# A hybrid decoder block: sums of squares of keys, queries and recurrence output in one fp32 pass, or in two fp32r passes

## The reference

```python
def rms_norm(x, gain):
    xf = x.astype(jnp.float32)
    xf = xf * lax.rsqrt(jnp.mean(xf * xf, axis=-1, keepdims=True) + EPS)
    return xf.astype(x.dtype) * gain
...
    q = rms_norm(q.reshape(B, S, G, HPG, DH), qk_gain[0]).transpose(0, 2, 3, 1, 4)
...
    k_s = rms_norm(heads(k_s), qk_gain[2])
...
    k_w = rms_norm(heads(k_w), qk_gain[3])
...
    o = rms_norm(o, out_gain.astype(jnp.float32)) * jax.nn.silu(g.astype(jnp.float32).reshape(B, S, HG_HEADS, HG_DV))
```

## Time and profile before

| what | value |
| --- | --- |
| time, median of 3 runs | 806.44 us (805.68 to 806.84) |
| time of the profiled execution | 806.03 us |
| its span, first to last instruction | 804.3 us |
| TensorE busy | 797.1 us (99%), granted clock 0.999 |
| VectorE busy | 396.2 us (49%) |
| ScalarE busy | 196.3 us (24%) |
| GpSimd busy | 489.1 us (61%) |

### The profile page before, as it was taken

One profiled execution on the slowest core, in us unless ns is written; L12 is line 12 of the kernel. 1 busy time (PEld: TensorE's weight loads), 2 busy tenths in 40 slices (PEclk: granted clock), 3 DMA queues, 4 the chain that ended last, 5 costly groups with the idle time before them and its releaser, 6 DMA issues.

```text
span 804.3 us, 12357 instructions
## 1 busy us (share of the span) xinstructions
PE 797.1 (99%) x4632; PEld 635.8 (79%) x4632; DVE 396.2 (49%) x565; ACT 196.3 (24%) x402; POOL 489.1 (61%) x325
## 2 busy tenths in 40 slices
PE   9999999999999999999999999999999999999998
PEld 7788878988787666577888888888888888888886
DVE  5794577734465445633457667661000476650000
ACT  6101753214311445725112222220000122210000
POOL 5666544676454755555666566676666676676663
PEclk9999999999999999999999999999999999999999
DMA  8244222233522010015223223233223223323320
GB/s 282 98 139 154 82 80 80 79 106 105 183 79 78 27 53 28 1 53 183 84 101 104 89 95 104 80 102 105 84 99 104 82 102 104 98 85 131 130 78 26
DMA packets 23549, 78.01 MB, mean 97 GB/s; under 512 B 2723, under 2 KB 3499, under 8 KB 23380
## 3 DMA queue, kind: packets, MB, share of 16 engines
q1 hardware_dynamic: 19964, 69.00, 25.8%
q10 hardware_dynamic: 3544, 8.44, 2.9%
HBM read 75.31 MB, written 4.21 MB: 99 GB/s over the span
## 4 chain that ended last, share of the span: by engine, by line
PE 96%; ACT 1%; POOL 1%; DMA 1%; DVE 1%; issue 0%; SPq 0%; DVEq 0%; POOLq 0%; ACTq 0%
PE bank L385 27%; PE bank L387 26%; PE bank L386 26%; PE bank L709 3%; PE bank L731 3%; PE bank L752 2%; PE bank L467 1%; PE bank L468 1%; PE bank L469 1%; PE bank L409 1%; ACT gates L1081 1%; PE bank L516 1%; DMA x<-in_xT 1%; POOL wsp L305 1%; PE bank L625 1%; PE bank L741 1%
## 5 line engine op out<-in xcount | busy, mean ns | idle before, releaser
L305 POOL TENSOR_TENSOR wsp<-wraw,wsp 128x1024 fp32r<-128x1024 f32 x124 | 305.8, 2466 | 10.3
L303 POOL TENSOR_SCALAR wsp<-wraw 128x1024 fp32r<-128x1024 f32 x124 | 135.3, 1091 | 243.7 <-PE bank L387 159.2
L385 PE MATMUL bank<-hhi,wsp 128*128 128x512 f32 x352 | 140.6, 399 | 0.9 <-POOL wsp L305 0.4
L386 PE MATMUL bank<-hlo,wsp 128*128 128x512 f32 x352 | 137.3, 390 | 0.0
L387 PE MATMUL bank<-hhi,wsp 128*128 128x512 f32 x352 | 137.3, 390 | 0.0
L385 PE MATMUL bank<-ghi,wsp 128*128 128x512 f32 x256 | 100.4, 392 | 0.0
L387 PE MATMUL bank<-ghi,wsp 128*128 128x512 f32 x256 | 99.7, 389 | 0.0
L385 PE MATMUL bank<-uhi,wsp 128*128 128x512 f32 x256 | 99.7, 389 | 0.0
L386 PE MATMUL bank<-glo,wsp 128*128 128x512 f32 x256 | 99.6, 389 | 0.0
L386 PE MATMUL bank<-ulo,wsp 128*128 128x512 f32 x256 | 99.6, 389 | 0.0
L387 PE MATMUL bank<-uhi,wsp 128*128 128x512 f32 x256 | 99.6, 389 | 0.0
(11 more groups left out here) (246 smaller groups left out, 1012.1 us busy)
## 6 DMA issues: line engine op xcount, KB each, us to landing
wraw<-in_w SPq DMA_DIRECT2D x126, 512.0 KB, 3.3
bias_skewed<-bias_lines ACTq DMA_DIRECT2D x1, 2048.0 KB
bias<-bias_skewed ACTq DMA_DIRECT2D x1, 2048.0 KB, 8.7
x<-in_xT ACTq DMA_DIRECT2D x1, 2048.0 KB, 8.1
out<-x ACTq DMA_DIRECT2D x8, 256.0 KB, 2.0
x<-in_xT SPq DMA_DIRECT2D x3, 512.0 KB, 6.6
x<-in_xT SPq DMA_DIRECT2D x2, 256.0 KB, 4.4
wraw<-in_w SPq DMA_DIRECT2D x4, 128.0 KB, 8.0
```

Of the source, the lines that this page charges most:

```text
L303: pool.tensor_scalar(whi[:, two, :], wraw[:, raw, :], 1.0, 0.0, ALU.mult, ALU.add).then_inc(w_hi, 1)
L305: pool.tensor_tensor(wlo[:, two, :], wraw[:, raw, :], whi[:, two, :].bitcast(F32), ALU.subtract).then_inc(w_split, 1)
L385: pe.matmul(out_, wh, mh, start=first, stop=False)
L386: pe.matmul(out_, wh, ml, start=False, stop=False)
```

## The change

The ten sums over 512 columns use fp32r matmuls. ScalarE squares into `sq` as before, waits for that, and copies the square into an fp32r tile `sq_hi` (rounding it). VectorE subtracts: `sq_lo = sq - sq_hi` (`square_low`). TensorE multiplies both by the matrix of ones (now an fp32r copy) into the same bank, the second adding to the first (`split_stat`), and waits for `sq_low` in place of `stat_in`. VectorE's ten subtractions are put in by hand: number n of the first six in turn n of the loop, behind `keep_near(n)` or `keep_32` and ahead of `norm`; 6 and 7 (for `st_o0`, `st_o1`) between `kcn` and `gelu(1)`; 8 and 9 in the loop of the heads. Before the first square ScalarE also waits for `raw_low`, since `sq_hi` lies where `raw_hi` was.

```diff
+            def split_stat(name, matrix):
+
+                i = split_stats[0]
+                pe.wait_ge(sq_low, i + 1)
+                to = claim(name)
+                pe.matmul(to[:], matrix, sq_hi[i // 6][:, i % 2, :], start=True, stop=False)
+                pe.matmul(to[:], matrix, sq_lo[i // 6][:, i % 2, :], start=False, stop=True).then_inc(stat_out, 1)
+                split_stats[0] += 1
...
-            stat("st_ks", pair_ones[:], sq[:, 0, :])
+            split_stat("st_ks", pair_r[:])
...
-                stat(f"st_o{h}", ones[:], sq[:, h % 2, :])
+                split_stat(f"st_o{h}", ones_r[:])
...
+            def square_split(raw):
+
+                i = squares[0]
+                if i >= 2:
+                    act.wait_ge(sq_low, i - 1)
+                if i == 0:
+                    act.wait_ge(raw_low, 2)
+                link(act.activation(sq[:, i % 2, :], raw, ACT.Square))
+                act.activation(sq_hi[i // 6][:, i % 2, :], sq[:, i % 2, :], ACT.Copy).then_inc(sq_high, 1)
                 squares[0] += 1
...
+            dve.tensor_copy(ones_r[:], ones[:])
+            dve.tensor_copy(pair_r[:], pair_ones[:])
...
+            def square_low(i):
+                dve.wait_ge(sq_high, i + 1)
+                dve.tensor_tensor(sq_lo[i // 6][:, i % 2, :], sq[:, i % 2, :], sq_hi[i // 6][:, i % 2, :].bitcast(F32),
+                                  ALU.subtract).then_inc(sq_low, 1)
...
                 if n == 6:
                     keep_64()
+                if n < 6:
+                    square_low(n)
...
             dve.sem_inc(kcn_ready, 1)
+            square_low(6)
+            square_low(7)
             gelu(1)
...
                 dve.tensor_tensor(o_, o_, gs[:, h, :], ALU.mult).then_inc(oa_f, 1)
+                if h < 2:
+                    square_low(8 + h)
```

More of the change, by code:

```diff
@@ L137, in build_block @@
         pt_high = [at("pt_high0", 116.5, [P, 2, 4, 256]), at("pt_high1", 178.5, [P, 2, 4, 256])]
+        ones_r = at("ones_r", 188.5, [P, P], F32R)
+        pair_r = at("pair_r", 189, [P, P], F32R)
+        sq_hi = [at("sq_hi", 190.5, [P, 2, S], F32R), at("sq_hi_o", 194.5, [P, 2, S], F32R)]
+        sq_lo = [at("sq_lo", 172.5, [P, 2, S], F32R), at("sq_lo_o", 198.5, [P, 2, S], F32R)]
         cst = at("cst", 204.5, [P, 336])
@@ L202, in build_block @@
         stat_in = sem("stat_in")
+        sq_high, sq_low = sem("sq_high"), sem("sq_low")
         stat_out = sem("stat_out")
@@ L409, in stat @@
                 pe.matmul(to[:, 0:n], matrix, squares, start=True, stop=True).then_inc(stat_out, 1)
+            split_stats = [0]
+            def split_stat(name, matrix):
[5 more added lines that the diff above has]
+                split_stats[0] += 1
             def first_projection(n, each_k):
@@ L572, in _ @@
             project("kw")
-            stat("st_ks", pair_ones[:], sq[:, 0, :])
+            split_stat("st_ks", pair_r[:])
             near_level(1)
             project("nq0")
-            stat("st_kw", pair_ones[:], sq[:, 1, :])
+            split_stat("st_kw", pair_r[:])
             near_level(2)
             project("nq1")
-            stat("st_q0", pair_ones[:], sq[:, 0, :])
+            split_stat("st_q0", pair_r[:])
             near_level(3)
             project("nq2")
-            stat("st_q1", pair_ones[:], sq[:, 1, :])
+            split_stat("st_q1", pair_r[:])
             near_level(4)
             project("nq3")
-            stat("st_q2", pair_ones[:], sq[:, 0, :])
+            split_stat("st_q2", pair_r[:])
             level_32()
@@ L589, in _ @@
             next(parts)
-            stat("st_q3", pair_ones[:], sq[:, 1, :])
+            split_stat("st_q3", pair_r[:])
             level_64()
@@ L653, in _ @@
             project("ga0")
-            stat("st_o0", ones[:], sq[:, 0, :])
+            split_stat("st_o0", ones_r[:])
             pe.wait_ge(csum, 2)
@@ L828, in _ @@
                     if j == 0:
-                        pe.wait_ge(stat_in, 13)
+                        pe.wait_ge(stat_in, 3)
                         pe.matmul(bank[2][:], ones[:], tmp[:], start=True, stop=True).then_inc(stat_out, 1)
@@ L932, in square @@
                     act.wait_ge(stat_out, squares[0])
-                act.activation(sq[:, squares[0] % 2, :], raw, ACT.Square).then_inc(stat_in, 1)
+                square_split(raw)
+            def square_split(raw):
[6 more added lines that the diff above has]
+                act.activation(sq_hi[i // 6][:, i % 2, :], sq[:, i % 2, :], ACT.Copy).then_inc(sq_high, 1)
                 squares[0] += 1
@@ L1017, in square_o @@
                 act.wait_ge(stat_out, 7 if h < 2 else 7 + h)
-                act.activation(sq[:, h % 2, :], bank[2 + h][:], ACT.Square).then_inc(stat_in, 1)
+                square_split(bank[2 + h][:])
             square_o(0)
```

## The result

| | before | after |
| --- | --- | --- |
| time, median | 806.1 us (6 executions, 805.68 to 806.84) | 814.49 us (6 executions, 813.40 to 817.18) |
| ratio | 1 | 1.0107 (95% interval 1.0092 to 1.0121) |
| profiled execution, its span | 806.03, 804.3 | 813.93, 812.2 |
| mean granted clock | 0.999 (profiled execution) | 0.994 to 0.998 (six executions) |

What follows compares the result with a forecast made beforehand. The prediction took TensorE, busy 797.1 of 804.3 us, to bound the kernel. Keys and queries +2.8, compressed values +1.7 and the other output sums 0 made +4.5: 810.9 us on the median, range 807.4 to 814.2.

Steps and rivals of the forecast that it cites:

- What bounds the kernel: Whole kernel: TensorE, busy 797.1 of 804.3 us, sets the time; VectorE's 49% says nothing about a given moment.
- The price of a pass: Each sum on TensorE: two fp32r matmuls with the switch take 0.55 instead of 0.95, 0.63 after a wait.
- The price of two SBUF inputs: VectorE's subtractions: each waits for the GpSimd operation that runs and makes the next one wait; 0.69 each when unhindered.
- Step 1: Keys and queries: waits of 4.83 for low parts, less 2.00 given back by the sums: +2.8 us.
- Step 2: Compressed values: two low parts push the gelu's second half behind GpSimd's next chunk, so `cmp_v` starts later: +1.7 us.
- Step 3: Last three output sums: no gain, since the next projection waits for the gate's bank that L1154 reads: 0 us.
- The sum: Whole kernel: 2.8 + 1.7 + 0 = +4.5, 810.9 us on the median.
- The rivals: Whole kernel, other outcomes: 801.8 (5%), 807.0 (12%), 808.9 (20%), 813.5 (18%); the forecast itself had 42%.
- The nearest in time, 813.5: Last query's sum: its low part misses the gap between GpSimd operations, VectorE and TensorE wait 2.6 longer: +7.1; 18%.
- Waits grow beyond 0.5 at the third to fifth sum: Keys' and queries' loop, sign of error in step 1: VectorE, not TensorE, would set the pace, norms underrated.

Runs made afterwards that it cites:

- keys alone: Kernel before, with only the six sums of keys and queries as two passes, the output's four left as fp32: 814.56 us, ratio 1.0101.
- output part alone: Kernel before, with only the four output sums as two passes, keys and queries left as fp32: 809.22 us, ratio 1.0031.
- control: Whole change, but the sum `st_q1` waits only for its high part and reads it twice, its low part left out: 817.61 us, ratio 1.0144.
- held sum: Kernel before, fp32 sums kept, with one added wait: `st_q0` also waits for VectorE's norm of the window keys: 807.93 us, ratio 1.0020.
- the last run: Whole change, with `square_low(2)` moved ahead of `advance(2)` and `square_low(7)` behind `gate("ga0")`: 810.81 us, ratio 1.0066.
- the tiny matmuls: Whole change plus 16 tiny fp32 matmuls on TensorE before its first low-part wait, bank claims moved ahead of these waits: 812.46 us, ratio 1.0072.
- one high sum: Whole change, but the sum `st_q0` waits only for its high part and reads it twice, its low part left out: 811.15 us, ratio 1.0067.

## Why the prediction was wrong

**What bounds the kernel**: right. VectorE's share of 49% hid that it was late at a few moments: two waits for low parts, the wait at L677 and a short one at `st_q0`.

**The price of a pass**: right. 0.55 was forecast and the pair with its switch took 0.54 where nothing held it.

**The price of two SBUF inputs**: right. The low part at 198.33 ran only when the L310 of 198.13 had ended, and the low part at 145.97, first by 0.13, made the L310 of 146.10 take 2.79 instead of 2.40. The Trainium skill, page "SBUF — State Buffer", section "Who interferes with whom", has such an exclusive lock; the trace agrees.

**Step 1**: its sum was right, 2.8 forecast and 2.6 found (806.9 against 804.3, keys alone). The waits at `st_ks` and `st_q3` were forecast at 2.07 each and show as 1.80 and 1.92 of idle time. For `st_q0` 0.39 were forecast; it came 7.63 after `st_kw`, where the sums without low parts take 7.34: 0.29. One term was loose: the text prices a subtraction at 0.69, the steps count 0.54 behind a lock, and the trace bears out the steps (104.09 for 104.12).

**Step 2**: +1.54 for +1.7, and for the reason given. Moving one low part takes it away (output part alone, 4.70 from `st_o0` to `cmp_v`; with the move, 2.75).

**Step 3**: right, 0; the bank binds.

**The sum** is the step that failed. It was made of waits and works as long as TensorE, once released, runs as before. Two terms were missing:
- The supply of instructions: 2.2. The prediction asked of each wait how long it is, and never whether the instructions behind it would be there in time. In the five traces with the gap behind a sum that waited (whole change, keys alone, control, held sum, and the last run, with two causes taken away) the packet starts 1.0 to 1.3 after that wait is met and the level goes on 2.4 to 3.0 after the packet starts. In before the packet starts at 116.3, so by the same 2.4 to 3.0 the block is there at 118.7 to 119.3, and the level needs it at about 119.6: a margin of under 1 that no idle time shows. The wait of `st_q0`, forecast at 0.39 and met at 119.2, used it up.
- The clock: 1.7 for each fall. The prediction said in so many words that the granted clock should stay at 0.999. Leaving aside the first 2 us, where every trace has a pause of 1.68, seven profiled kernels have pauses of 1.67 or more, 20 in all; 12 have a stretch of 3.41 at the lower level behind them, which begins 0.4 to 1.5 after the pause. No kernel without such a pause has one before the last 2 us. With four such pauses the whole change runs at 0.994 to 0.998.

Taken off the spans, at 1.7 for each fall and the gap's own length, they leave about the span that was forecast, 808.8: the whole change 812.2 - 1.7 - 2.2 = 808.3, with the tiny matmuls 811.7 - 1.7 - 1.2 = 808.8, with one high sum 810.2 - 1.7 = 808.5, the control 814.9 - 5.1 - 1.7 = 808.1.

**The rivals**: none had the right cause. The nearest in time, 813.5, was wrong in its mechanism (the last low part did get its gap), so the range nearly held the time for a reason that did not occur. "Waits grow beyond 0.5 at the third to fifth sum" was named as a sign of an error; the delay did come there, but not from VectorE.

**Shown and not shown.** Shown: one wait that is met just ahead of its sum makes the gap (held sum), and taking the wait of `st_q0` away removes it (one high sum), with a control for each; the break is at a block's end, and the block's packet starts late. Not shown: the mechanism inside. That TensorE's sequencer stands at the wait and therefore asks for the next block later fits all five traces, but no row shows the request. It does not cover all of them: in the run with the tiny matmuls the gap came behind a sum that did not wait (its low part had ended at 110.9, the sum started at 111.97, the packet at 112.25). And with one high sum a wait of 0.17 at `st_q1` made no gap where 0.20 made one in the last run; the packet had started at 121.9 in the one and at 128.1 in the other, both times for the block that begins in the middle of `near_level(4)`, and why it was so late in the other, where TensorE shows no idle time between 121.3 and 127, is open. Open too is why a pause of 1.8 at `st_ks` is followed by a fall of the clock in one execution and not in another: the pauses and the falls stand side by side in the traces, and no run changed one alone.

Of the versions that leave nothing out none beats the kernel before: the best, with three of the ten sums, is level with it.

## What to carry to other kernels

A new wait on the engine that bounds the time can cost more than its length: here the packet of instructions for the burst behind it came late too (1.75 for a wait that itself cost next to nothing), and a pause may bring the clock down behind it. So price a pause of 2 us on a TensorE that is otherwise full at 2 to 4, compare where a level or burst breaks off with the ends of the blocks of 256 instructions, and look for idle time "issue" and for falls of the granted clock before explaining what is left by anything else. And half an engine's time being free is no place for an operation: in each order tried here, subtractions of 0.7 delayed copies or decays for which TensorE was already waiting, or nearly so, or came late themselves.

## What the runs showed of the hardware

- TensorE can outrun its supply of instructions: a level's 128 matmuls and 128 weight loads pass in 1.3, and where TensorE stood waiting for a block it went on 2.4 to 3.0 after the packet of 16 KB started. The Trainium skill, "Runtime: NRT & Kernel Launch", "Instruction fetch mechanics", calls the cost of crossing a block mostly hidden, because instructions go out more slowly than blocks come in. In most levels here that is so, but in seven of the fourteen traces a level stopped for 0.2 to 2.2.
- A wait that was met 0.2 ahead of its instruction, and shows no idle time, cost 1.75 (held sum), and the same at the next sum nothing (806.48 against 806.18).
- Matmuls of 512 columns start 0.23 apart at the full clock and 0.43 apart in the stretches of 3.41 at half of it. Such stretches followed pauses of 1.67 to 2.22, in 12 of 20 cases, and none followed those of 1.55 and 1.18, nor that of 1.04 that every trace has at about 380.
